# Delta stage: the first inverse factor transposed by VectorE instead of TensorE

## The reference

```python
L = jnp.where(strict, jnp.einsum('bhnid,bhnjd->bhnij', kb, k) * decay, 0.0)
rhs = jnp.concatenate([v * beta[..., None], kb * jnp.exp(gc)[..., None]], -1)
sol = lax.linalg.triangular_solve(L + jnp.eye(C, dtype=L.dtype), rhs, left_side=True,
                                  lower=True, unit_diagonal=True)
```

## Time and profile before

| What | Value |
|---|---|
| device time, median of 3 runs | 2718.54 us (2718.34 to 2718.98) |
| span of the profiled execution, first to last instruction | 2717.0 us |
| TensorE busy | 2678.4 us |
| VectorE busy | 1909.8 us |
| ScalarE busy | 1212.6 us |
| GpSimd busy | 854.2 us |

### The profile page before, as it was taken

The page is one execution under the profiler, slowest core; times in us unless marked ns, Lnnn a source line. Parts: engine busy times, 40 slices in busy tenths (PEclk is TensorE's granted clock), DMA queues, the critical chain, the costliest instruction groups (busy, mean ns, idle before and its releaser), DMA issues.

```text
span 2717.0 us, 45293 instructions
## 1 busy us (share of the span) xinstructions
PE 2678.4 (99%) x17387; PEld 2250.4 (83%) x17387; DVE 1909.8 (70%) x2190; ACT 1212.6 (45%) x1572; POOL 854.2 (31%) x646
## 2 busy tenths in 40 slices
PE   6999999999999999999999999999999999999998
PEld 4798998899898888888888888889777778888887
DVE  1476777787787687666666666588999997655554
ACT  2355455545546445333333333354433334444344
POOL 1076676676667412600000000004565550000000
PEclk9999999999999999999999999999999999999999
DMA  9966666676665676666666666655555556666664
GB/s 364 354 219 207 227 225 204 223 239 200 224 229 188 219 223 228 189 187 186 187 190 188 190 186 186 185 162 172 171 179 170 161 173 187 192 186 186 192 202 155
DMA packets 283976, 552.53 MB, mean 203 GB/s; under 512 B 16882, under 2 KB 54323, under 8 KB 282675
## 3 DMA queue, kind: packets, MB, share of 16 engines
q1 hardware_dynamic: 263488, 473.49, 56.5%
q0 software_dynamic: 19472, 76.06, 7.4%
q10 hardware_dynamic: 866, 0.80, 0.1%
HBM read 548.19 MB, written 2.10 MB: 203 GB/s over the span
## 4 chain that ended last, share of the span: by engine, by line
PE 96%; DMA 2%; DVE 1%; SPq 1%; ACT 0%; issue 0%; DVEq 0%
PE pg L1220 40%; PE pd L1220 18%; PE pg L936 13%; PE pg L923 6%; PE pg L1207 4%; PE pg L955 3%; PE pd L849 2%; DMA wr<-in_gdn_w_in 1%; PE pd L1096 1%; PE pd L1078 1%; PE pd L1415 1%; PE pd L1428 1%; DMA arena<-in_mod_w 1%; PE pg L849 1%; PE pd L1027 1%; PE pd L1010 1%
## 5 line engine op out<-in xcount | busy, mean ns | idle before, releaser
L2341 DVE TENSOR_TENSOR wl<-wr,wh 128x1024 fp32r<-128x1024 f32 x615 | 773.7, 1268 | 453.7 <-ACT wh L1818 451.2
L1818 ACT ACTIVATE wh<-wr 128x1024 fp32r<-128x1024 f32 x616 | 652.8, 1061 | 936.2 <-PE pg L1220 590.3
L662 POOL TENSOR_TENSOR wl<-wr,wh 128x1024 fp32r<-128x1024 f32 x195 | 478.9, 2458 | 366.3 <-ACT wh L1599 231.3
L1220 PE MATMUL pg<-wh,hh 128*128 128x512 f32 x1344 | 529.8, 394 | 0.3 <-DVE hl L2414 0.3
L1220 PE MATMUL pg<-wl,hh 128*128 128x512 f32 x1344 | 527.3, 392 | 0.0
L1220 PE MATMUL pg<-wh,hl 128*128 128x512 f32 x1344 | 525.7, 391 | 0.0
L1599 ACT ACTIVATE wh<-wr 128x1024 fp32r<-128x1024 f32 x216 | 227.7, 1057 | 356.4 <-PE pg L936 196.4
L1220 PEld LDWEIGHTS pg<-wh,hh 128*128 128x128 f32 x1344 | 252.6, 188 | 59.1 <-DVE wl L2341 2.4
L936 PE MATMUL pg<-hh,wh 128*128 128x256 f32 x1024 | 300.7, 294 | 0.8 <-ACT arena L1659 0.8
L1220 PEld LDWEIGHTS pg<-wh,hl 128*128 128x128 f32 x1344 | 252.5, 188 | 56.3
L1220 PEld LDWEIGHTS pg<-wl,hh 128*128 128x128 f32 x1344 | 252.3, 188 | 53.9
(11 more groups left out here) (446 smaller groups left out, 4727.3 us busy)
## 6 DMA issues: line engine op xcount, KB each, us to landing
wr<-in_w_in SPq DMA_DIRECT2D x224, 512.0 KB, 3.8
wr<-in_ffn_w_gu SPq DMA_DIRECT2D x176, 512.0 KB, 3.8
wr<-in_gdn_w_in SPq DMA_DIRECT2D x128, 512.0 KB, 4.1
arena<-in_mod_w POOLq DMA_DIRECT2D x60, 1024.0 KB, 6.7
wr<-in_ffn_w_down SPq DMA_DIRECT2D x88, 512.0 KB, 4.6
arena<-in_mod_w SPq DMA_DIRECT2D x32, 1024.0 KB, 13.7
wr<-in_gdn_w_in SPq DMA_DIRECT2D x128, 256.0 KB, 3.1
wr<-in_gdn_w_out SPq DMA_DIRECT2D x56, 512.0 KB, 4.5
```

Of the source, the lines that this page charges most:

```text
L662: nc.gpsimd.tensor_tensor(wl[c % RING][:], wraw[c % 4], wh[c % RING][:].bitcast(F32), ALU.subtract)\
L1220: m = nc.tensor.matmul(halves(bank)[:, h, :], act[x][:, k0 + k, h * P:(h + 1) * P], w[s][:, k, :], skip_group_check=True, start=(first and ...
L1818: a(wh[c % 4][:], wraw[c % 4], ACT.Copy).then_inc(s_hc, 1)
L2341: v.tensor_tensor(wl[c % 4][:], wraw[c % 4], wh[c % 4][:].bitcast(F32), ALU.subtract).then_inc(s_lc, 1)
```

## The change

- `flip_blocks` is gone. The masked first factor is now written to `Us`, the right half of `Ub` (free at that time), in its natural place: block `b` of matrix `n` in partition half `b`. VectorE subtracts it from the identity there and transposes it into `Tc` with its own transpose operation, which works on 32x32 blocks; the factor is zero outside 2x2 blocks, so this is the whole transpose.
- The first level uses the crossed order of the later levels. The half of the blocks that already stand on the right partitions are read from `Us`; ScalarE copies the other half across the partitions to `Uc` (count `u1`), behind the second half of `vtok`.
- ScalarE's second `vtok` copy waits for TensorE's transposes of v (`vt1`) and no longer for VectorE. TensorE doesn't wait for `lm` any more, and before the second product of level 2 it waits for `u1`.

```diff
-PEO = order("ssq", "rows", "gram", "ktok", "t2", "x2", ...
+PEO = order("ssq", "rows", "gram", "ktok", "vt1", "x2", ...
-VO = order("qn", "qkn", "dt", "lt", "lm", "at", "tc", "uc", ...
+VO = order("qn", "qkn", "dt", "lt", "lm", "at", "us1", "tc", ...
...
+        Us = Ub[:, :, 64:P]
# TensorE
-                V("lm")
                 Ac("kg")
-                def crossed(s, b, n):
-                    return (b, slot(n)) if s == 2 else (n % 2, 4 * b + n // 2)
+                def crossed(b, n):
+                    return n % 2, 4 * b + n // 2
+                def u_block(s, b, n):
+                    half, i = crossed(b, n)
+                    r = slice(64 * half, 64 * half + 64)
+                    return Us[r, n, :] if s == 2 and half == b else Uc[r, n // 2 if s == 2 else i, :]
-                flip_blocks(pd[0], Uc, slot)
...
                     V(f"x{s}")
-                    if s > 2:
-                        Ac(f"u{s // 2}")
-                    else:
-                        V("uc")
-                        Ac("vtok")
+                    Ac(f"u{s // 2}")
# ScalarE
-                V("tc")
+                PEw("vt1")
                 a(vtok[:, VH:8, :] ...
+                V("us1")
+                a(Uc[0:64, 0:4, :], heads(Us)[64:P, :, 0, :], ACT.Copy)
+                a(Uc[64:P, 0:4, :], heads(Us)[0:64, :, 1, :], ACT.Copy).then_inc(s_a, 1)
# VectorE
-                    m = v.tensor_tensor(by_n(four(Uc[r])), heads(lTb[r, :, r]), ...
+                    m = v.tensor_tensor(Us[r], lTb[r, :, r], ...
...
-                PEw("t2")
-                done(v.tensor_tensor(heads(Tc), identc..., by_n(compact(pd[0])), ALU.subtract))
                 dve.wait_ge(s_v, bv + VO["lm"])
-                done(v.tensor_tensor(Uc, identc.unsqueeze(1).broadcast_to([P, 8, 64]), Uc, ALU.subtract))
+                done(v.tensor_tensor(Us, identc.unsqueeze(1).broadcast_to([P, 8, 64]), Us, ALU.subtract))
+                dve.wait_ge(s_v, bv + VO["us1"])
+                done(v.transpose(Tc, Us))
```

More of the change, by code:

```diff
@@ L48, in order @@
     return {n: i + 1 for i, n in enumerate(names)}
-PEO = order("ssq", "rows", "gram", "ktok", "t2", "x2", "tx2", "u2", "x4", "tx4", "u4", "x8",
+PEO = order("ssq", "rows", "gram", "ktok", "vt1", "x2", "tx2", "u2", "x4", "tx4", "u4", "x8",
             "tx8", "u8", "x16", "tx16", "u16", "x32", "tx32", "u32", "x64", "ux64", "v0", "md0", "s", "o0", "r",
             "qs", "v1", "o1", "md1")
-VO = order("qn", "qkn", "dt", "lt", "lm", "at", "tc", "uc", *[f"{a}{s}" for s in LEVELS for a in ("x", "t")],
+VO = order("qn", "qkn", "dt", "lt", "lm", "at", "us1", "tc", *[f"{a}{s}" for s in LEVELS for a in ("x", "t")],
            "x64", "u64", "md0", "o0", "rhs1", "o1", "oz", "md1", "on", "og")
-AO = order("rnq", "rn", "exp", "kg", "vtok", "z", *[f"u{s}" for s in LEVELS], "v0", "s", "qs", "v1", "qkv", "rstd")
+AO = order("rnq", "rn", "exp", "kg", "vtok", "u1", "z", *[f"u{s}" for s in LEVELS], "v0", "s", "qs", "v1", "qkv", "rstd")
 GO = order("rowm")
@@ L1077, in x_step @@
                             r = slice(64 * b, 64 * b + 64)
-                            m = nc.tensor.matmul(block(pd[par], *crossed(s, b, n)), lTb[r, n, r], Tc[r, n, :],
+                            m = nc.tensor.matmul(block(pd[par], *crossed(b, n)), lTb[r, n, r], Tc[r, n, :],
                                                  start=True, stop=True)
@@ L1086, in delta @@
                     V(f"x{s}")
-                    if s > 2:
-                        Ac(f"u{s // 2}")
-                    else:
-                        V("uc")
-                        Ac("vtok")
+                    Ac(f"u{s // 2}")
                     par ^= 1
                     for b, n in each_block():
-                        half, i = crossed(s, b, n)
+                        half, i = crossed(b, n)
                         r = slice(64 * half, 64 * half + 64)
-                        m = nc.tensor.matmul(block(pd[par], b, slot(n)), Uc[r, i, :], Xc[r, i, :], start=True, stop=True)
+                        m = nc.tensor.matmul(block(pd[par], b, slot(n)), u_block(s, b, n), Xc[r, i, :], start=True, stop=True)
                     m.then_inc(s_pe, 1)
@@ L2222, in delta @@
                     r = slice(64 * b, 64 * b + 64)
-                    m = v.tensor_tensor(by_n(four(Uc[r])), heads(lTb[r, :, r]),
-                                        m1t[r, 0:64].unsqueeze(1).unsqueeze(1).broadcast_to([64, 4, 2, 64]), ALU.mult)
+                    m = v.tensor_tensor(Us[r], lTb[r, :, r], m1t[r, 0:64].unsqueeze(1).broadcast_to([64, 8, 64]),
+                                        ALU.mult)
                 done(m)
@@ L2231, in delta @@
                 yield
-                PEw("t2")
-                done(v.tensor_tensor(heads(Tc), identc.unsqueeze(1).unsqueeze(1).broadcast_to([P, 4, 2, 64]),
-                                     by_n(compact(pd[0])), ALU.subtract))
                 dve.wait_ge(s_v, bv + VO["lm"])
-                done(v.tensor_tensor(Uc, identc.unsqueeze(1).broadcast_to([P, 8, 64]), Uc, ALU.subtract))
+                done(v.tensor_tensor(Us, identc.unsqueeze(1).broadcast_to([P, 8, 64]), Us, ALU.subtract))
+                dve.wait_ge(s_v, bv + VO["us1"])
+                done(v.transpose(Tc, Us))
                 yield
```

## The result

The changed kernel takes 2729.98 us (median of 5 runs, 2727.78 to 2730.11); the kernel before took 2718.98 beside it (2718.34 to 2719.32). The ratio is 1.004, with a 95% interval of 1.0029 to 1.005: slower, by 11.0 us. The profiled execution is the run of 2727.78, with a span of 2726.2, 9.2 more than before. New are L2230 (the subtraction on `Us`), L2232 (the transpose) and L1701, L1702 (the crossed copies).

The account below looks back on a forecast made before the run. TensorE, busy 99% of the span, was taken to bound the kernel, with VectorE and GpSimd taking turns. Six middle iterations +24.6, first +3.3, last -1.8 gave +26.1 on 2718.5: 2745 us, range 2700 to 2752 (8 in 10).

Parts of the forecast that it names:

- TensorE's part: Each delta-loop iteration: transposes at L1059 removed, 1.17 us; two first-level products moved to four quarters, 0.92 us; 2.09 saved.
- the lead: TensorE's saving in each delta-loop iteration: 2.09 us, 16.7 in eight iterations.
- the nearest row: L2236, nearest by place to VectorE's added transpose: 2.19 us, which would have the transpose held behind GpSimd's second operation.
- the third rival: VectorE's transpose held behind GpSimd, 1.7 us wait before level 2, +5.6 per middle iteration: 2755 us; chance 0.07.
- The walk: One iteration followed through all engines' timelines: TensorE waits 6.2 us less lead 2.09, each middle iteration 4.1 us longer.
- the first L2087 pair ... ends at 278.40 and 279.18: VectorE's first pair waits for GpSimd until 277.85, then its halves end there, ahead of GpSimd's third operation.
- a turn lost one pair later: GpSimd goes between the halves of VectorE's second pair, 281.99 to 284.25; TensorE waits 1.6 us for L2246.
- waits of 6.2: TensorE's waits in us per middle iteration, on L2246 and L2241, after lost VectorE turns in successive levels.
- the second rival: Turn lost once per iteration, later levels back in step: 0.5 us gained per iteration, 2715 us; chance 0.11.
- my sum: Six middle iterations 24.6 us, first 3.3, last -1.8: together +26.1 us on the span.
- where I had 3.3: First iteration: 4.1 us longer less a wait of 0.8 already paid, so 3.3 us.
- a gain of 1.8: Last iteration: one wait of 0.3 us lost, the rest of TensorE's lead kept, -1.8 us.

Follow-up runs that it names:

- the kernel with the quarters alone: Changed kernel, but TensorE transposes the first factor as before and VectorE subtracts twice; four-quarter first level and ScalarE's crossed copies stay: 2741.09 us, ratio 1.0085.
- the version with the pairs two steps later: Changed kernel with VectorE's modulation-sum pairs two level-loop steps later, GpSimd's weight loads moved along, the first load one chunk earlier: 2706.54 us, ratio 0.9956.
- the ten experiments with full pairs: Edits of the changed kernel that keep VectorE's modulation-sum operations at 512 columns, not cut to 2; measured from 2706.54 to 2823.87 us.
- the kernel with GpSimd held: Changed kernel with GpSimd's third operation of each iteration but the last held until VectorE's first two modulation-sum pairs are done: 2739.16 us, ratio 1.0079.

## Why the prediction was wrong

The direction was right, the size was not: +11.0 us where I forecast +26.1, and the place of the loss was another.

- TensorE's part held. L1059 is gone, L1076 and L1090 take 0.69, and the lead without waits is 2.13 (forecast 2.09).
- The transpose took 0.71 us against the 0.69 that I had put down; the copies 0.42 each, 0.84 against 0.8. GpSimd's second operation runs from 279.4 to 282.20, across the whole transpose, and does not hold it up. The Trainium skill (GPSIMD Engine Reference, Key points) was right in this against the nearest row, and the third rival falls.
- The walk held up to the turn that decided it. Shifted by 4.35 us (this iteration starts that much later), it had the subtraction's end at 279.90 (measured 279.95), GpSimd's second operation's at 282.20 (282.20), the first half of the pair's at 282.75 (282.75), and GpSimd ready behind its DMA issue at 283.00 (282.96).
- **The step that failed** is "the first L2087 pair ... ends at 278.40 and 279.18": that its second half, 0.25 us ahead of GpSimd (278.40 against 278.65; by the record it was 0.17), keeps its turn. It lost it, in every middle iteration. I took from no row how far ahead is enough, and the earlier trace rows hold a warning: the half that lost its turn there is recorded from 181.35, 0.02 ahead of GpSimd's operation of 181.37. I had a turn lost one pair later, to GpSimd's fourth operation, which I had ready 0.35 ahead of that second half.
- From this the rest follows. Lost at the second pair, the turn would have left TensorE with a lead that meets the next turn, and so on: waits of 6.2. Lost at the first, it costs one wait of 2.02, and a middle iteration at full clock is 96.74 - 94.46 = 2.28 longer than one without any wait, 0.15 more than the whole lead; L1090 starts at 286.79 - 4.35 = 282.44, 0.41 later than in the earlier trace rows, and is 0.46 shorter. From there each engine stands as before, and no turn is lost again. That is the second rival (lost once, then back in step), at another place. The six middle iterations pay 3.4 us together (four of 0.12 to 0.15, two of 1.44 and 1.47), not 24.6. Some 2.7 of the 3.4 are the lower clock in two iterations, for which my sum had no term.
- A row of waits like the one that I forecast for all middle iterations did come, in the first iteration (2.40, 0.84, 1.16, 0.84, 1.17 and 0.14; 4.1 us longer where I had 3.3) and in the kernel with the quarters alone. In the first iteration GpSimd's operation went ahead of the first half of the second pair (recorded from 188.87, 3.67 us), not between its halves.
- The last iteration and what follows lost 1.4 where I expected a gain of 1.8; it has a wait of 2.23 at the second product of level 4, not of level 2, and the lower clock behind it. The mask stands there behind a subtraction of 128x1024 on VectorE (L2302) that takes 6.30 beside two operations of GpSimd, and took 3.76 in the kernel before.
- That the sign came out right is partly luck: a middle iteration ends within 0.15 of where it was, and what makes the kernel slower is the first iteration and three drops of the clock; the lost turn of a middle iteration only takes the gain away.

The span's 9.2 us: 0.3 ahead of the stage, 4.1, 3.4 and 1.4. The runs that were timed lie up to 2.3 above the profiled one, at a mean granted clock of 0.992 to 0.993 where it has 0.994.

The one cause that stays argued and not shown by an experiment of its own is why 0.17 us was not enough; the last section has what the records say.

## What to carry to other kernels

Work taken off the engine that is busy for 99% is only time if the order of the other engines' work survives when that engine runs ahead: here operations of two of them took turns instead of running side by side, and a lead of 2 us changed who came first. Before such a change is costed, list for each operation that takes turns with another how far ahead of it it starts; where that is less than the lead, move the uncritical operation out of the stretch along with the change, as the version with the pairs two steps later does (2706.5). A little idle work in the right place is a cheap test for this: if it makes the kernel faster, the loss is one of order and not of work.

## What the runs showed of the hardware

**Directly behind a DMA issue of its own, GpSimd's operation took the turn from pairs recorded ahead of it.** Counted over the records of the kernel before, the changed one and the ten experiments with full pairs, between 130 and 950 us: a half of a pair that is recorded as started inside a GpSimd DMA issue took its normal 0.74 to 0.75 us in all 397 cases where GpSimd's subtraction did not follow the issue directly, and lost its turn (3 us and more) in 50 of 53 where it did, though it was recorded up to 0.7 us ahead of the subtraction. Where the subtraction had waited for ScalarE, a half recorded 0.1 to 1.0 us ahead of it kept its turn each time (841 cases), and of 11 recorded less than 0.1 ahead 8 lost it. The Trainium skill (SBUF — State Buffer, section "SBUF: two separate sides") says that whichever starts first gets the shared ports for the whole instruction. By the recorded starts the 50 cases and the 8 speak against it. The Trainium skill (Perfetto Trace Analysis, GPSIMD Engine Instruction) also says that a GpSimd instruction's span in a profile is not to be relied on; the claim may then come ahead of the record, which no run here shows by itself.

**TensorE's clock fell after some of the new waits.** Windows of the changed kernel behind the wait of 2.03 that ends at 480.25:

```profile
480.25:480.90 0.65, 0.65 (x33) 0.58 (x33) 0.65 (x1) 0.52 (x2) 0.65 (x1) 1.00 1.05 410
480.90:484.30 3.40, 3.40 (x20) 3.40 (x17) 3.24 (x4) 0.00 (x0) 1.41 (x2) 0.51 0.93 298
484.30:490.00 5.70, 5.70 (x98) 5.33 (x100) 4.29 (x9) 1.86 (x3) 2.61 (x2) 0.99 0.67 229
```

The granted clock is 0.51 for 3.4 us, the lower level of 1.2 GHz, and then back. It costs 98.06 - 96.71 = 1.35 us (the third iteration, with an equal wait of 2.03, takes 96.71 at 1.00). Three of the eight iterations show it, behind waits of 2.02 to 2.23, and seven of the kernel with GpSimd held, each with a wait of 2.23 to 5.09; the kernels with no wait in the middle iterations show 1.00 in theirs. Why waits of equal length are followed by it or not stays open.
